# Bias tiles read in wanted order from a scratch that holds the scaled distance table 128 times, without the stage that flips them on TensorE

## What is computed

```python
dist = W + i[:, None] - j[None]
bias = rel_b.reshape(G, HPG, REL_BUCKETS)[:, :, _t5_bucket(dist)]
logits = jnp.einsum('bnqghd,bnkgd->bghnqk', q, kk, ...) * scale
logits = jnp.where(mask, logits + bias[:, :, None], -jnp.inf)
```

## Time and profile before

| | us |
|---|---|
| median of 3 runs | 2818.17 |
| lowest and highest run | 2817.51, 2819.13 |
| span of the profiled execution | 2815.3 |
| TensorE busy in it | 2644.5 |
| VectorE, ScalarE busy in it | 1284.8, 1059.5 |

### The profile page before, as it was taken

How to read it: one execution, slowest core, us unless ns; L and a number is a source line. 1 busy time by engine, 2 the same in 40 slices (tenths; PEclk the granted TensorE clock), 3 DMA queues, 4 the chain that set the end, 5 groups by cost and what they waited for, 6 DMA issues and landing times.

```text
span 2815.3 us, 40283 instructions
## 1 busy us (share of the span) xinstructions
PE 2644.5 (94%) x16574; PEld 1948.3 (69%) x16574; DVE 1284.8 (46%) x2355; ACT 1059.5 (38%) x1748; POOL 69.0 (2%) x28
## 2 busy tenths in 40 slices
PE   8999999999999999999989899999888999998996
PEld 8988988899898988889888654433336864433433
DVE  5565554755756565475677651111116653111112
ACT  4444563444444465344457631111114442111110
POOL 0001000100100100010010000000000000000000
PEclk9999999999999999999999999999999999999999
DMA  9645633565463853446354289999996229999997
GB/s 308 220 118 157 215 97 115 195 198 193 155 206 107 228 164 105 162 158 204 109 180 130 87 339 416 420 421 421 421 418 210 91 96 421 421 420 421 421 421 290
DMA packets 315366, 695.37 MB, mean 247 GB/s; under 512 B 58224, under 2 KB 243440, under 8 KB 266032
## 3 DMA queue, kind: packets, MB, share of 16 engines
q1 hardware_dynamic: 312000, 682.09, 66.1%
q10 hardware_dynamic: 3184, 10.69, 1.2%
HBM read 691.65 MB, written 1.08 MB: 246 GB/s over the span
## 4 chain that ended last, share of the span: by engine, by line
PE 64%; DMA 19%; DVE 10%; ACT 5%; issue 2%; SPq 1%; ACTq 0%; DVEq 0%
PE ps L295 26%; DMA ring<-in_moe_w_gate 8%; PE ps L2619 7%; PE ps L827 7%; DMA slots_over_xT<-in_moe_w_gate 6%; DMA moe_slots<-in_moe_w_gate 5%; PE ps L1605 3%; PE ps L2669 3%; PE ps L1645 3%; DVE weight_parts L226 3%; PE ps L334 2%; PE ps L306 2%; ACT weight_parts L218 1%; PE ps L2555 1%; SPq L2521 1%
## 5 line engine op out<-in xcount | busy, mean ns | idle before, releaser
L295 PE MATMUL ps<-xT_upper,weight_parts 128*128 128x256 f32 (+1 forms) x4656 | 843.4, 285 | 17.8 <-DVE arena L2241 7.5
L226 DVE TENSOR_TENSOR weight_parts<-ring,weight_parts 128x1024 fp32r<-128x1024 f32 x479 | 611.2, 1279 | 489.8 <-ACT weight_parts L218 489.2
L295 PEld LDWEIGHTS ps<-xT_upper,weight_parts 128*128 128x128 f32 (+1 forms) x4656 | 717.2, 189 | 41.5 <-DVE weight_parts L226 13.7
L218 ACT ACTIVATE weight_parts<-ring 128x1024 fp32r<-128x1024 f32 x479 | 504.0, 1055 | 533.4 <-PE ps L295 321.0
L295 PE MATMUL ps<-xT_lower,weight_parts 128*128 128x256 f32 (+1 forms) x2328 | 649.8, 283 | 1.9 <-DVE xT_lower L988 1.5
L295 PEld LDWEIGHTS ps<-xT_lower,weight_parts 128*128 128x128 f32 (+1 forms) x2328 | 437.3, 189 | 3.6 <-DVE xT_lower L988 2.8
L2619 PE MATMUL ps<-ring,bias_tiles 128*64 128x512 f32 x1024 | 243.1, 595 | 27.9 <-DMA ring<-in_moe_w_gate 16.0
L2914 DVE TENSOR_TENSOR arena<-ps,arena 128x512 f32<-128x512 f32 x32 | 22.1, 692 | 475.2 <-ACT arena L2782 475.2
L827 PE MATMUL ps<-weight_parts,hidden_upper 128*128 128x512 f32 x704 | 218.3, 391 | 4.4 <-DVE hidden_lower L880 4.4
L2619 PEld LDWEIGHTS ps<-ring,bias_tiles 128*64 128x64 f32 x1024 | 78.9, 137 | 182.9 <-issue 126.2
L2782 ACT ACTIVATE arena<-ps 128x512 f32<-128x512 f32 x32 | 19.2, 599 | 494.9 <-PE ps L2619 494.9
(11 more groups left out here) (335 smaller groups left out, 3191.0 us busy)
## 6 DMA issues: line engine op xcount, KB each, us to landing
ring<-in_ffn_w SPq DMA_DIRECT2D x132, 1024.0 KB, 5.2
ring<-in_moe_w_up SPq DMA_DIRECT2D x64, 1024.0 KB, 26.8
ring<-in_moe_w_gate SPq DMA_DIRECT2D x64, 1024.0 KB, 26.3
ring<-in_moe_w_down SPq DMA_DIRECT2D x64, 1024.0 KB, 26.7
moe_slots<-in_moe_w_up SPq DMA_DIRECT2D x48, 1024.0 KB, 26.6
moe_slots<-in_moe_w_down SPq DMA_DIRECT2D x40, 1024.0 KB, 26.6
slots_over_xT<-in_moe_w_gate SPq DMA_DIRECT2D x32, 1024.0 KB, 27.5
moe_slots<-in_moe_w_gate SPq DMA_DIRECT2D x32, 1024.0 KB, 26.2
```

The source lines that it names most:

```text
L218: act.activation(self.part(n, 0), cut(self.stream.slot(pos)), ACT.Copy).then_inc(self.upper_done, 1)
L226: dve.tensor_tensor(self.part(n, 1), cut(self.stream.slot(pos)), self.part(n, 0).bitcast(F32), ALU.subtract).then_inc(self.split, 1)
L295: m = pe.matmul(out[0:rows, :], w[of_w][:, k, :], c.xTp[of_x][:, k, :], start=(at == 0), stop=(at == len(steps) - 1))
```

## The change

The scratch becomes 16 x 128 x 512 numbers and holds each head's row 128 times. The read takes partition p from copy p, at offset 127 - p of that copy (p x 511 + 127 in all), so that the tiles arrive in the wanted order. The factor 1/SCALE moves into the one-hot matrix and the mask, on the host. The flipping stage, its matrix and the matrix's load are gone; the waits that the stage had made for the constants are put into the first mixer, together with one of VectorE for the tiles.

```diff
-CONSTANTS = 7 + 4 * DEPTH
+CONSTANTS = 6 + 4 * DEPTH
...
-        self.scratch = nc.dram_tensor("bias_scratch", [16, 512], F32, kind="Internal").ap()
+        self.scratch = nc.dram_tensor("bias_scratch", [16, P, 512], F32, kind="Internal").ap()
...
-        sp.dma_start(flip_matrix(c), a["c_flip"]).then_inc(c.const_landed.sem, 16)
...
         act.wait_ge(c.setup_dve.sem, 2)
-        act.dma_start(c.scratch, brow[0:16, :]).then_inc(c.stored.sem, 16)
+        act.dma_start(c.scratch, window(brow[0:16, :], 0, [[0, P], [1, 512]])).then_inc(c.stored.sem, 16)
...
 def load_bias_tiles(c, sp):
     E_v = c.E[:, 0:16 * S].rearrange("p (h n) -> p h n", h=16)
     sp.wait_ge(c.stored.sem, 16)
-    sp.dma_start(E_v, bass.AP(c.scratch.tensor, 0, [[1, P], [512, 16], [1, S]])).then_inc(c.bias_landed.sem, 16)
+    sp.dma_start(E_v, bass.AP(c.scratch.tensor, P - 1, [[511, P], [P * 512, 16], [1, S]])).then_inc(c.bias_landed.sem, 16)
...
-def flip_bias_stage(c):
...
@@ mix_projection_stage, TensorE, ahead of the first projection
-        if c.aux_act.issued:
-            pe.wait_ge(c.aux_act.sem, c.aux_act.issued)
-            pe.wait_ge(c.aux_dve.sem, c.aux_dve.issued)
+        if l == 0:
+            pe.wait_ge(c.const_landed.sem, 16 * CONSTANTS)
...
@@ attention stage, VectorE
-            for sig in (P_.log_act, P_.kept_act, P_.kept_dve, P_.cmp_hidden, c.rows, c.aux_act):
+            for sig in (P_.log_act, P_.kept_act, P_.kept_dve, P_.cmp_hidden, c.rows):
                 dve.wait_ge(sig.sem, sig.issued)
+            if l == 0:
+                dve.wait_ge(c.const_landed.sem, 16 * CONSTANTS)
+                dve.wait_ge(c.bias_landed.sem, 16)
...
@@ build
-            if l == 0:
-                flip_bias_stage(c)
...
@@ constants
-    k["c_flip"] = np.eye(P, dtype=f)[::-1].copy()
-    k["c_onehot"] = onehot * (dist >= 0)
+    k["c_onehot"] = onehot * (dist >= 0) / f(SCALE)
-    k["c_bmask"] = bmask
+    k["c_bmask"] = bmask / f(SCALE)
```

More of the change, by code:

```diff
@@ L717, in bias_tile @@
     return c.E[:, h * S:(h + 1) * S]
-def flip_matrix(c):
-    return c.E[:, 17 * S + 2048:17 * S + 2048 + P]
 def load_bias_tiles(c, sp):
```

## The result

The changed kernel takes 2835.72 us (median of 4 runs, 2833.47 to 2836.30) against 2817.84 us of the kernel before beside it (4 runs): ratio 1.0059, 95% interval 1.0047 to 1.0071. It is slower by 17.9 us; forecast was 8.9. The kernel before, profiled again, drifted by up to 3.2 us (experiment 6), so shifts of one or two microseconds mean nothing by themselves. The profiled execution of after took 2835.3 us, its span is 2833.5 us (2815.3 before).

A forecast was written before the change was run, and what follows sets the result against it. TensorE, busy 2644.5 of 2815.3 us, was taken as the bound. Removed stage -11.5, store's stall +18.7 and lower clock +1.7 gave +8.9 us on 2818.2: 2827.1 us, range 2806 to 2848, the forecast's own range 2823 to 2835.

The forecast's parts named there:

- rival C: First feed-forward: slow store also holds up weight pieces 4 to 7, piece 4 landing at 63.6 us; 2839.7 us, chance 0.22.
- Removed stage, -11.5 us: Layer 0 mixer: without the flip's 32 matmul passes, the way to the projection's rounding and compression matmuls shortens by 11.5 us.
- The twin: Second layer's same norm and projections without the flip: 6.48 us to the rounding, 36.58 us to the compression matmuls.
- Removed or moved at no cost: One 64 KB load goes, 1/SCALE moves to host constants, waits move to the first mixer; bias tiles there by 100 us.
- The store's duration: First feed-forward: 4.19 MB from 16 partitions at 91 GB/s takes 46.1 us plus 1.4, landing at 63.6 us.
- All weight pieces from number 8 on are queued behind the same wait: SyncE's queue: piece 8, third chunk's down weights, waits for the store, landing at 76.4 us, needed by 57.7.
- Stall +18.7 us: First feed-forward: TensorE idles 18.7 us, once, because weight piece 8 lands at 76.4 us instead of by 57.7.
- the clock's, +1.7: After the first feed-forward's stall, TensorE's granted clock is 0.71 for 5 us and 0.95 for 5 more: +1.7 us.
- A: The store runs at the engines' rate, 11.4 us, mostly covered; 2806.7 us, to 2810 if piece 4 is late; chance 0.20.
- B: Store at 127 GB/s, half the 64-partition rate: 33.0 us, landed at 50.5, stall 5.6 us; 2814.0 us, chance 0.20.
- D: Store rate in proportion to partitions: 66.0 us, landed at 83.5, stall 38.6 us; 2847.0 us, chance 0.08 with worse.
- the signs to look for: No flip row; store landing after 47.5 us; long SyncE wait; 19 us TensorE idle before third chunk; clock under 1.00 after.

The follow-up runs named there:

- experiment 6: The kernel before, unchanged, profiled a second time: 2817.97 us, one run.
- experiment 1: Changed kernel with the old one-copy store and old read, so no flip and bias tiles left with partitions in reverse: 2810.28 us, ratio 0.9968.
- experiments 9 to 12: 16 or 40 tiny matmuls at TensorE's program head: one-copy kernel with backward reads 2806.66 and 2809.24 us, kernel before 2819.35, changed kernel 2831.87.
- Experiment 2: Changed kernel with the bias read and its wait moved behind all weight pieces of the first feed-forward on SyncE's queue: 2830.49 us, ratio 1.0040.
- experiment 3: Changed kernel storing as many bytes in the same 2 KB runs, but zeros from 128 partitions instead of the table's 16: 2813.01 us, ratio 0.9982.
- experiment 5: Kernel before, flip kept, with only the store of 128 copies added: 2842.19 us, ratio 1.0087.
- after_pad16: Changed kernel with 16 tiny matmuls put at the head of TensorE's program: 2831.87 us, ratio 1.0043.

## Why the prediction was right in sign and short in size

The measured 2835.7 us lies in the range of 2806 to 2848, but just outside the forecast's own range of 2823 to 2835, and nearer to rival C's 2839.7 than to the 2827.1.

- **Removed stage, -11.5 us:** right to 0.1 us where it lies (23.5 to 12.0). The twin was the right ruler: 6.48 and 36.58 us came out to the hundredth of a microsecond. At the end of the program the removal alone is worth 7.5 us (experiment 1). The sentence that failed is "Downstream nothing is tied to absolute time": true of data, not of the instruction stream. With the flips' instructions gone, TensorE breaks off in a later norm, and that costs some 3 to 4 us (experiments 9 to 12).
- **Removed or moved at no cost:** right. The tiles landed at 75.2 us, long before 333.7 us, their first use.
- **The store's duration:** 46.1 + 1.4 = 47.5 us forecast, 46.5 measured. The closeness is luck in part, since two errors cancel. DMA queue of the store in the changed kernel, 21.6 to 62.4 us, that is all of its transfer (no packet of it runs before 21.6 us):

```profile
q10 hardware_dynamic: 2064, 4.19, 76.6%
```

The transfer took 40.8 us where 46.1 were forecast, at 103 GB/s and not 91, and it began 5.7 us after its issue, where 1.4 us were allowed for everything beside the bytes. The rate in the middle is 0.39 MB in 4 us, 98 GB/s. The Trainium skill (SBUF — State Buffer, Door 1: The DMA port swizzle) gives 104 GB/s for these partitions; the trace agrees within 1% over the whole and within 6% in the middle, beside other traffic and for a store. By that figure the store takes 40.3 us, an estimate; with the 1.4 us it would have been 5 us short of the 46.5, and those are the late start.

- **"All weight pieces from number 8 on are queued behind the same wait":** here the mechanism failed. SyncE reached that wait when it was over (66.27 against 62.4 us). In its place: pieces 4 to 7, issued long before, crawled at the store's packet rate (piece 6 for 21.0 us), and SyncE's later issues with them. Experiment 2 takes the wait away from the pieces and leaves +12.7 us of 17.9; experiment 3 keeps it, and TensorE has no stall.
- **Stall +18.7 us:** 15.3 + 4.4 = 19.7 us measured. So close a sum by the wrong piece is luck in part: the first stall ends with the store, whose end was forecast well, and the second behind piece 8, which SyncE issued only after that. "The stall is paid once" failed with it. The other three kernels with this store at this place stalled for 14.6 to 18.0 us, in part for other pieces. The term mis-sized is the clock's, +1.7: it was 3.8 us, since two idles cost it twice. To the end of the first feed-forward, 20.4 us were forecast and 23.5 came; by whole runs the store costs 24.0 us (experiment 5).
- **Rival C** had the sharing right and the price wrong: it took the engine to be lost to the other queue while a slow packet runs, so that piece 4 would land with the store. Piece 4 came at 31.7 us, 0.6 ahead of its need as forecast; the pieces get one packet for each of the store's. Against the chance of 0.22 it stands as the mechanism that decided. The Trainium skill (DMA: Bandwidth & Descriptors, Queues, rings and completion order) says that an engine goes round its queues by packets; the trace agrees, 190 to 189 and 381 to 376. The page counts a packet as about 9 to 17 descriptors; here the two queues stay even run for run, of 2 or of 1 KB, within 3 in every microsecond from 40 to 48 us, while nine runs of the store would hold an engine for 9 x 0.30 = 2.7 us at a time. With it I could have put a time on C. Piece 4 and piece 6 are 1024 runs each and piece 5, down weights in runs of 4 KB, is 256: 2304 in all against the store's 2048, so piece 6 lands about when the store ends. That is what happened (61.2 and 62.4 us).
- **A, B and D** are out: the store landed 46.5 us after its issue, not under 28, and at 62.4 us, neither at 50.5 nor at 83.5.
- **The sum:** +8.9 forecast, +17.9 measured: 3.6 us too little for the store (24.0 against 20.4), 4.0 us too much for the removal (11.5 against 7.5), the last 1.4 us unassigned and within the runs' spread. Of the signs to look for, three held (no row of the flip, landing after about 47 us, granted clock down behind the idle), and two did not: SyncE's long wait and where TensorE idles. The test for rival C, an idle before 40 us for piece 4, fails in the changed kernel's profile and holds in those of experiments 2 and 5 and of after_pad16 (2.9 us until 37.0 us). All four carry the same store at the same place, so the test was drawn too narrow: it hung on how much of piece 4 was through when the store began.

## What to carry to other kernels

A DMA that touches few partitions costs all queues on its engines: work out for each transfer beside it how many packets it needs while the slow one lasts, not only who waits for the slow one. Before a copy is multiplied in memory to save a reordering, look whether the reader can run through it backward; here it costs nothing. And when a removal's gain shrinks in a place that the edit doesn't touch, look for idle time that ends on nothing but issue, and test it with a few useless instructions ahead.

## Not expected of the hardware

- A 4.19 MB store in runs of 2 KB out of 16 partitions lands after 44.2 to 46.5 us in five kernels, each time beside weight loads; out of 128 partitions after 22.9 us, beside the same weight pieces. A 2 KB packet holds its engine 0.30 us in the one and 0.084 us in the other.
- Two queues of unlike speed share an engine one packet for one (188 to 188 in 4 us), so that the fast queue drops from 424 to 49 GB/s. The issuing engine is held too: four issues of SyncE took 22.18 us in place of 9.28.
- A program with 64 instructions more at its head runs a later stretch 4 us faster (504.8 to 501.1 us in the changed kernel), with one instruction load fewer (135 in place of 136).
- Backward reads of a tile by VectorE take as long as forward ones (median 353 against 351 ns for 96 operations).
- Portions of 1.7 us of clock go in the middle of full work, at places that differ in part from one execution to the next. What sets them is open.
